# Expert layers: 48 own tokens on the split tile in place of 64, and 336 dense tokens in place of 320

## The reference, cut to what matters

```python
act = jax.nn.gelu(einsum('td,ted->te', x, u_tab[eidx])) * gate
out = einsum('te,ted->td', act, v_tab[eidx])
```

## Time and profile before

| | |
|---|---|
| median of three runs | 4307.02 us |
| profiled execution | 4311.3 us, span 4309.2 us |
| TensorE matmul busy | 3888.6 us (90%) |
| VectorE busy | 3093.1 us (72%) |
| GpSimd busy | 1910.4 us (44%) |
| mean granted TensorE clock | 0.955 |

### The profile page before, as it was taken

The page is one execution under the profiler, slowest core; times in us unless marked ns, Lnnn a source line. Parts: engine busy times, 40 slices in busy tenths (PEclk is TensorE's granted clock), DMA queues, the critical chain, the costliest instruction groups (busy, mean ns, idle before and its releaser), DMA issues. The chain is left out here.

```text
span 4309.2 us, 46101 instructions
## 1 busy us (share of the span) xinstructions
PE 3888.6 (90%) x16342; PEld 2310.8 (54%) x16342; DVE 3093.1 (72%) x6176; ACT 687.7 (16%) x1432; POOL 1910.4 (44%) x1654
## 2 busy tenths in 40 slices
PE   8986889997899999999989997999888999999997
PEld 3643646775444444444347875577744444444442
DVE  6747535898877777777764137489988777777777
ACT  4122411163000000000012122103600000000000
POOL 0002300076677777766600000002866767777673
PEclk9997899998999999999989999999989999999999
DMA  4212741259999999999931104013899999999996
GB/s 183 85 47 99 270 177 40 73 174 315 382 409 419 420 420 420 420 418 411 420 125 58 69 20 120 27 55 117 257 402 376 420 419 420 420 416 420 414 420 277
DMA packets 375714, 1169.30 MB, mean 271 GB/s; under 512 B 35833, under 2 KB 120281, under 8 KB 364042
## 3 DMA queue, kind: packets, MB, share of 16 engines
q0 software_dynamic: 184960, 679.58, 38.9%
q1 hardware_dynamic: 107856, 445.02, 26.9%
q10 hardware_dynamic: 82684, 41.95, 3.4%
HBM read 1116.99 MB, written 48.37 MB: 270 GB/s over the span
## 5 line engine op out<-in xcount | busy, mean ns | idle before, releaser
L606 PE MATMUL banks<-h_dense_T,blocks 128*128 128x320 f32 x4096 | 1139.1, 432 | 0.0
L425 POOL DMA_INDIRECT expert_rows<-in_pk_u_dram,expert x640 | 832.3, 1301 | 356.1 <-DVE own_dots L891 173.2
L654 PE MATMUL banks<-blocks,picked_T 128*128 128x512 f32 x2048 | 990.2, 628 | 0.0
L606 PEld LDWEIGHTS banks<-h_dense_T,blocks 128*128 128x128 f32 x4096 | 776.9, 190 | 387.3 <-issue 98.5
L916 DVE SCALAR_TENSOR_TENSOR acc<-expert_rows,expert_weight,acc 128x1024 f32<-128x1024 f32 x628 | 793.9, 1284 | 253.1 <-DMA expert_rows<-in_pk_v_dram,expert 248.4
L425 POOL DMA_INDIRECT expert_rows<-in_pk_v_dram,expert x640 | 803.6, 1256 | 340.3 <-DVE acc L916 176.6
L891 DVE CUSTOM_DVE_ANT_0 expert_rows<-expert_rows,h_rows 128x1024 f32<-128x1024 f32 x640 | 775.1, 1225 | 246.3 <-DMA expert_rows<-in_pk_u_dram,expert 242.0
L654 PEld LDWEIGHTS banks<-blocks,picked_T 128*128 128x128 f32 x2048 | 384.8, 198 | 615.8 <-issue 615.8
L645 PE MATMUL banks<-blocks,picked_T 128*64 128x512 f32 x1024 | 292.3, 648 | 215.4 <-DVE picked_T L877 215.3
L449 ACT ACTIVATE dense_act<-banks 128x320 f32<-128x320 f32 x246 | 107.8, 438 | 2117.0 <-PE banks L606 2108.5
L413 POOL TENSOR_SCALAR expert_rows<-iota,picked_T 128x128 f32<-128x128 f32 x320 | 209.8, 678 | 443.7 <-ACT picked_T L455 396.2
(11 more groups left out here) (522 smaller groups left out, 3960.4 us busy)
## 6 DMA issues: line engine op xcount, KB each, us to landing
blocks<-in_pk_u_turned_dram SPq DMA_DIRECT2D x256, 512.0 KB, 6.5
blocks<-in_pk_v_dram SPq DMA_DIRECT2D x256, 512.0 KB, 6.6
ada_block<-in_ada_rest_dram SPq DMA_DIRECT2D x32, 1280.0 KB, 7.7
gates_dram<-shared ACTq DMA_DIRECT2D x40, 1024.0 KB, 5.5
shared<-gates_dram SPq DMA_DIRECT2D x32, 1280.0 KB, 10.5
blocks<-in_pk_w_q_dram SPq DMA_DIRECT2D x32, 512.0 KB, 3.6
expert_rows<-in_pk_u_dram,expert POOLq DMA_INDIRECT x640, 12.9
expert_rows<-in_pk_v_dram,expert POOLq DMA_INDIRECT x640, 13.5
```

Of the source, the lines that this page charges most:

```text
L425: pool.indirect_dma_start(out=rows[:, r % RING, :], out_offset=None, in_=table, in_offset=bass.IndirectOffsetOnAxis(ap=idx[:, at_:at_ + 1] ...
L606: mm = pe.matmul(dense_dots(c), u[:, k * P:(k + 1) * P], HT[:, k, 0:DENSE], start=(k == 0), stop=(k == KD - 1))
L654: mm = pe.matmul(ps[:, at_:at_ + HALF], wt[:, c % WEIGHED, z * P:(z + 1) * P], v[:, half_ * HALF:(half_ + 1) * HALF], start=(c == 0), stop ...
```

## The change

- `OWN` is 48. The two copies of the 48 own tokens lie on partitions 16 to 63 and 64 to 111. The gathers of unit 0 are still 64 of u and 64 of v, and each brings 96 rows in place of 128. `H[:, 2, :]` and the gate buffer are cleared first.
- `DENSE` is 336: every dense dot has 336 columns, the spread has 336 tokens, and the gate table is written in 21 pieces in place of 20.
- The sums of the split tile cover 96 tokens (80 dense ones and 16 whose weights are zero): the 64-token part as before, and a 32-token part as four matmuls of 32 tokens by 256 features, side by side in the array, into bank 5.
- The expert numbers and gates of the own tokens are now made in place and moved to the two copies by four small DMAs of ScalarE's queue, in place of four small VectorE instructions.
- At the end, four additions of 32 partitions by 256 and one multiplication by the gate row follow on each other, where one multiplication stood.

```diff
-OWN = 64
-WAYS = P // OWN
+OWN = 48
+WAYS = 2
+OWN_FIRST = P - OWN
+OWN_BLOCK = P // WAYS
+COPY_AT = (OWN_BLOCK - OWN, OWN_BLOCK)
+COPIES = slice(COPY_AT[0], COPY_AT[1] + OWN)
 DENSE = ND * P - OWN
+SUMMED = 352
-SPLIT_PARTS = ((0, 64, 4), (64, 32, 5)) if OWN == 32 else ((0, 64, 4),)
+SPLIT_PARTS = ((0, 64, 4), (64, 32, 5))
...
+            pool.memset(rows[:, 8:10, :], 0.0).then_inc(slots_set, 1)
...
+                some = slice(0, P) if u else COPIES
+                if kind == "u" and u:
+                    pool.wait_ge(idx_ready, u)
+                elif kind == "u":
+                    pool.wait_ge(own_moved, 16 * 2 * WAYS)
...
                     pool.indirect_dma_start(
-                        out=rows[:, r % RING, :], out_offset=None, in_=table,
-                        in_offset=bass.IndirectOffsetOnAxis(ap=idx[:, at_:at_ + 1], axis=0),
+                        out=rows[some, r % RING, :], out_offset=None, in_=table,
+                        in_offset=bass.IndirectOffsetOnAxis(ap=idx[0:some.stop - some.start, at_:at_ + 1], axis=0),
                     ).then_inc(row_in[r % RING], 16)
...
+            act.wait_ge(own_set, 2)
+            for q in range(WAYS):
+                copy, some = slice(COPY_AT[q], COPY_AT[q] + OWN), slice(q * OWN_STEPS, (q + 1) * OWN_STEPS)
+                act.dma_start(idx[q * OWN:(q + 1) * OWN, 0:OWN_STEPS], own_idx[OWN_FIRST:P, some]
+                              ).then_inc(own_moved, 16)
+                act.dma_start(own_gate[copy, :], picked[OWN_FIRST:P, ND - 1, 2, some]
+                              ).then_inc(own_moved, 16)
...
+                if c < WEIGHED:
+                    line.then(dve.memset(wt[:, c, DENSE:SUMMED], 0.0))
...
-                dve.tensor_tensor(wt[:, c % WEIGHED, :], activation_of(c),
+                dve.tensor_tensor(wt[:, c % WEIGHED, 0:DENSE], activation_of(c),
                                   gate_of[g % 2][:, :, c % KEYS_A_GROUP], ALU.mult
                                   ).then_inc(weighed, 1)
...
+                for n, (first, size, bank) in enumerate(SPLIT_PARTS):
                     width = D * size // P
+                    some = slice(first, first + size)
                     for q in range(P // size):
+                        here, to = part_of(first, size, q), slice(q * width, (q + 1) * width)
+                        part = ps[here:here + size, bank * HALF:bank * HALF + width]
+                        if n:
+                            line.count(dve.tensor_tensor(folded[some, to], part, folded[some, to],
+                                                         ALU.add))
+                        else:
+                            line.count(dve.tensor_tensor(acc[some, 0, to], part, g_row[some, 1, to],
+                                                         ALU.mult))
+                line.settle()
+                line.count(dve.tensor_tensor(acc[P - OWN_BLOCK:P, 0, :], folded[P - OWN_BLOCK:P, :],
+                                             g_row[P - OWN_BLOCK:P, 1, :], ALU.mult))
...
+            dve.memset(H[:, NR, :], 0.0).then_inc(own_clear, 1)
...
+            sp.wait_ge(own_clear, 1)
+            for at in COPY_AT:
+                sp.dma_start(H[at:at + OWN, NR, :], h_of(ND - 1)[OWN_FIRST:P, :]
```

More of the change, by code:

```diff
@@ L269, in experts @@
                "hot_second", "spread", "spread_out", "gates_put0", "gates_put1", "gates_got0",
-               "gates_got1", "dots_out", "weighed", "idx_ready", "row_used", "own_dots", "own_gelu", "own_sum", "fold_done", "fold_out",
+               "gates_got1", "dots_out", "weighed", "idx_ready", "row_used", "own_set", "own_moved", "slots_set", "own_dots", "own_gelu", "own_sum", "fold_done", "fold_out",
                "g_free", "g_in", *names, *blocks) as (
@@ L301, in experts @@
         block = ctx.enter_context(nc.Block())
-        wt = cols[:, :, :, :].rearrange("p z a t -> p (z a t)")[:, 0:WEIGHED * DENSE].rearrange(
-            "p (b t) -> p b t", t=DENSE)
+        wt = cols[:, :, :, :].rearrange("p z a t -> p (z a t)")[:, 0:WEIGHED * SUMMED].rearrange(
+            "p (b t) -> p b t", t=SUMMED)
         at_part = act_w[:, UNIT_AT[1]:UNIT_SLOTS].rearrange("p (a s) -> p a s", a=2).bitcast(U32)
@@ L327, in experts @@
         batches = DENSE // BATCH
+        own_idx = idx[:, UNIT_AT[2]:UNIT_AT[2] + SLOTS]
         def scores(c):
@@ L518, in _ @@
                         ins = act.activation(
-                            folded[P - OWN:P, q * OWN_WIDTH:(q + 1) * OWN_WIDTH],
-                            ps[q * OWN:(q + 1) * OWN, fold_bank:fold_bank + OWN_WIDTH], ACT.Copy)
+                            folded[P - OWN_BLOCK:P, q * OWN_WIDTH:(q + 1) * OWN_WIDTH],
+                            ps[q * OWN_BLOCK:(q + 1) * OWN_BLOCK, fold_bank:fold_bank + OWN_WIDTH],
+                            ACT.Copy)
                     ins.then_inc(fold_out, 1)
@@ L829, in experts_of @@
                 if i == ND - 1:
[L830 to L836, removed]
+                    dve.scalar_tensor_tensor(
+                        out=own_idx, in0=picked[:, i, 0, :], scalar=float(P),
+                        in1=picked[:, i, 1, :], op0=ALU.mult, op1=ALU.add).then_inc(own_set, 1)
                     yield
@@ L847, in experts_of @@
                 if i == ND - 1:
[L848 to L852, removed]
+                    dve.sem_inc(own_set, 1)
                 yield
@@ L937, in add_split @@
                 dve.wait_ge(fold_out, 1)
-                line.count(dve.tensor_tensor(acc[P - OWN:P, 0, :], folded[P - OWN:P, :],
-                                             g_row[P - OWN:P, 1, :], ALU.mult))
-                for first, size, bank in SPLIT_PARTS:
+                for n, (first, size, bank) in enumerate(SPLIT_PARTS):
                     width = D * size // P
+                    some = slice(first, first + size)
                     for q in range(P // size):
[L943 to L947, removed]
+                        here, to = part_of(first, size, q), slice(q * width, (q + 1) * width)
[9 more added lines that the diff above has]
+                                             g_row[P - OWN_BLOCK:P, 1, :], ALU.mult))
                 line.settle()
@@ L982, in normalize @@
                 dve.tensor_tensor(h, h, shift[:, g, :], ALU.add).then_inc(h_ready, 1)
[L984 to L988, removed]
+            copy = COPY_AT[0]
+            line.count(dve.memset(own_gate[:], 0.0))
+            line.count(dve.memset(fold[:, 0:copy], 0.0))
+            line.count(dve.tensor_tensor(fold[:, copy:OWN_BLOCK], ident[:, copy:OWN_BLOCK],
+                                         ident[:, COPY_AT[1]:COPY_AT[1] + OWN], ALU.add))
+            line.settle()
             for c in range(CODES):
@@ L2511, in _ @@
             sp.wait_ge(h_ready, ND)
-            for q in range(WAYS):
-                sp.dma_start(H[q * OWN:(q + 1) * OWN, NR, :], h_of(ND - 1)[P - OWN:P, :]
+            sp.wait_ge(own_clear, 1)
+            for at in COPY_AT:
+                sp.dma_start(H[at:at + OWN, NR, :], h_of(ND - 1)[OWN_FIRST:P, :]
                              ).then_inc(first_blocks, 16)
```

22 lines of the change are left out of this document (12 added, 10 removed).

## The result

The kernel after takes 4426.56 us, the median of four runs (4415.11 to 4433.15), against 4309.83 us for the kernel before (four runs too; the 4307.02 of the table is its first three). The ratio is 1.0265, 95% interval [1.0248, 1.0281]: slower by 2.65%. The forecast was 4321 us, and its range ended at 4360. The profiled execution took 4422.58 us with a span of 4420.8, 111.6 us more than before, at a mean granted clock of 0.961 against 0.955. The clock is no part of the loss.

A forecast was written before the change was run, and what follows sets the result against it. DMA was taken to bound each pair (9.81 us), with 0.9 us of room in TensorE. Terms summed to +6.9 us a layer, +14 for both: 4311.3 profiled becomes 4325, less 4.3 for the median, 4321 us; range 4286 to 4360.

The forecast's parts named there:

- the relief in DMA: Unit 0's two phases: smaller gathers cut a pair's DMA time from 9.8 to 8.1 us, at 420 GB/s.
- lead: Phase of v rows, 12 pairs from about 3460: VectorE runs ahead of PE by some 19 us, up to three chunks.
- Chunks 33 to 107: 75 pairs of dots and sums in the second loop: 9.78 us each, 733.5 against 743.5, -10 us a layer.
- the first 25 chunks: Start of the loop, bound by VectorE: lighter gathers save 0 to 3 us, clears and L877 cost about 1; -1.
- the end of the spread to the first sums: Last gate write, 21.11 us beside the first gathers: a quarter smaller gathers give -2 us (0 to -5).
- two bounds that collide: Rival, chance 0.08: PE's and DMA's waits add, a pair takes 10.1 us; +31 a layer, 4369 us.
- No relief: Rival, chance 0.15: smaller gathers save no DMA time, pairs stay 9.91 us; +20 a layer, 4351 profiled, 4347 median.
- TensorE's prices: TensorE without waits: a pair 9.75 us, a chunk of sums 5.23, the new 32-token part 0.59.
- The rival without a change of shape: Rival, chance 0.20: the 32-token part adds only 0.43 us to a chunk of sums; -9.5 a layer, 4288 us median.
- early dots and end of the layer: Outside the loop, per layer: 16 dots before the last transposes +3.4 us, four additions at the end +1.8.
- The spread: Ahead of the loop, per layer: 16 more tokens +4.1 us, five dots +1.1, ScalarE's four DMAs +0.5 (0 to 1.5).
- the last 20 chunks: End of the loop, sums only: from 97.05 us to 20 x 5.23 = 104.6, +7.5 a layer.

The follow-up runs named there:

- e3: The kernel before, with unit 0's gathers bringing 96 rows to partitions 16 to 111 and two ring slots cleared; 4384.07 us, ratio 1.0182.
- e1: The kernel after, with unit 0's gathers at 128 rows again and expert numbers made for all 128 partitions first; 4343.06 us, ratio to before 1.0073.
- e8: The kernel before, with 48 full gathers of 128 rows each way in unit 0 in place of 64; 4229.3 us, ratio 0.9811.
- e4: The kernel before, with unit 0's gathers bringing 64 rows to partitions 0 to 63; 4334.61 us in one run.
- e5: The kernel before, with unit 0's gathers bringing 64 rows to partitions 32 to 95; 4221.89 us in one run.

## Why the prediction was wrong

The sign was right and TensorE's part was right; the size was wrong through one step. The sign came by another cause than the forecast's: it had the kernel some 14 us slower through TensorE's work, with a relief from the gathers, and the runs put some two thirds of the loss on the gathers (73 of 111.6 us).

- *The step that failed* is "one in unit 0's phases needs 5.5 x 0.13 = 0.72 MB less, 3.4 MB or 8.1 us", the relief in DMA. It took the rate of 420 GB/s as given and let only the bytes change. The rate fell to 289 (282 in e3). Chunks 33 to 49 take 195.7 / 17 = 11.5 us each, not 9.78, so VectorE has no lead but a debt. Chunks 33 to 107 were forecast at -10, or -5 when they are counted rightly (below), and came at +30; the first 25 chunks at -1 and came at +11 to +14; the end of the spread to the first sums at -2 and came at +11.7 in layer 1 (in layer 0 -0.4), e1 having +5.8 there. In layer 1 the last gate write took 28.5 us to land instead of 21.1, and DMA moved 290 GB/s around it instead of 388. Why layer 0 shows nothing stays open, and two profiles can't tell this part from the scatter.
- *The rivals.* By the number "two bounds that collide" was the nearest, 4369, still 57 us short. Its mechanism did not come: chunks 50 to 107 took 572.8 / 58 = 9.88 us each, not 10.1. "No relief", 79 us short, had the right suspicion, that gathers of 96 rows need be no cheaper than full ones, and the wrong lower bound: that they can at worst bring nothing. Its reason, a busiest engine or port with as many rows as before, no run shows. The relief was bounded by none at all on one side and a DMA time of 8.1 us a pair on the other, and never below nothing. Its sum of 4351 profiled is 9 too high (see the miscounted chunk), 4342 when counted rightly; e1, where the relief is absent by construction, had a span of 4347.8.
- *TensorE's prices* held to 0.02 us: 9.75 and 9.73, 5.23 and 5.21, 0.59 and 0.57. The rival without a change of shape (0.43) is refuted.
- *Ahead of the loop*: early dots and end of the layer together +4.5 (796.1 to 800.7 from the last chunk of layer 0 to the spread) for a forecast of 5.2. The spread +5.6 for 5.7. In it PE's second group waits 2.99 us for ScalarE where it waited 0.74, so ScalarE's copies were probably nearer to 2 us on the path than to 0.5, and the other parts smaller; no run separates them.
- *The miscounted chunk*: the stretch from 3453.00 to 4196.48 holds 304 records of L645, four a chunk, so 76 chunks: 75 pairs and the first chunk of sums alone, which starts at 4191.84 (lines below, from the kernel before). The prediction divided the whole by 75. A pair took 738.3 / 75 = 9.84 us and not 9.91, and the last stretch, 229 records at twelve a chunk, holds 19 chunks and not 20. The pairs should have read 733.5 - 738.3 = -5 in place of -10, and the last 20 chunks 104.6 - 101.7 = +3 in place of +7.5 (measured over 19: +1.9). The two errors cancel, so the forecast of the sum is untouched, by luck. In "no relief", which left the stretch as it was and added the +7.5, the chunk counts twice, 4.6 us a layer.

```profile
4187.44 4.47 PE L606 MATMUL banks<-h_dense_T,blocks 128*128 128x320 f32 x16
4191.84 1.08 PE L645 MATMUL banks<-blocks,picked_T 128*64 128x512 f32 x4
4192.85 3.70 PE L654 MATMUL banks<-blocks,picked_T 128*128 128x512 f32 x8
4196.48 1.08 PE L645 MATMUL banks<-blocks,picked_T 128*64 128x512 f32 x4
```

- *Signs named in advance*: GB/s below 420 in unit 0's phases came, but with DMA fully busy, which the text did not ask for and which is what tells slower packets from less demand. VectorE's waiting for PE after 3460 did not come (4.8 us in the loop). PE's wait for the weights was to fall under 60 us a loop and fell to 79.1. The sign set against the lead, 50 us of that wait between chunk 33 and 107, did not show either (32.0), though there was no lead: a longer pair hid the waits in chunks 50 to 107 as well.

## What to carry to other kernels

In this kernel a DMA that writes fewer partitions was not simply a smaller DMA. Its loops run at 420 GB/s, and with gathers onto 96, 112 or the lower or upper 64 partitions it took 4335 to 4449 us against 4310 with full ones; the transfers beside them slowed too, a 4 KB packet from 159 to between 229 and 263 ns. Save bytes by issuing fewer full gathers (e8, with 48 in place of 64: 4229 us), or measure several ranges of partitions: with 64 rows at 32 to 95 it took 4222 us, at 0 to 63 4335, half of unit 0's rows being left out in both. When a forecast divides bytes by a rate, ask whether the edit changes the rate, and let the bound of an untested shape reach beyond zero; and before moving work from one saturated resource to another, price both: here 81 us against 73.

## What the runs showed that was not expected

- A 4 KB packet on a queue that the change does not touch took 159 ns, 229 beside 96-row gathers at 16 to 111, and 263 beside 64-row gathers at 0 to 63, with all 16 engines busy (share 1.03 to 1.04).
- Beside 64 rows at 32 to 95 its median stays 159 and its mean is 181; 64 rows at 0 to 63 or at 64 to 127 give 263 and 262. e4 and e5 differ by 113 us.
- By row count the totals do not run evenly: 64 rows in the lower half 4335, 96 rows at 16 to 111 4384, 112 rows 4449, 128 rows 4310 us.
- Four small copies on ScalarE's queue took 0.55 to 0.66 us each to issue, where the writes of the gate table on that queue took 0.37 to 0.42, one of them in rows 10.
